# Placing expert 0's rows by matrix products, in a two-layer mixture-of-experts backbone on one Trainium2 core

## The reference, cut to what matters

```python
h2l = modulate(rms_norm(xl, norm_ffn[l]), sh2, sc2)
xl = xl + g2 * moe_ffn(h2l, w_router, b_router, *experts)
# moe_ffn, per token:
#   aff = sigmoid(tok @ w_router); best group of 4 experts; best 2 experts in it -> e_idx, w_sel
#   xs = tok_pad[row_tok]                      # rows sorted by expert, in blocks of 128
#   hb = silu(xb @ w_gate[e]) * (xb @ w_up[e]); ys = hb @ w_down[e]
#   out[token] += ys * row_w
```

## Time and profile before

| | |
|---|---|
| median of the runs | 2365.96 us |
| the profiled execution | 2363.81 us |
| its span in the profile | 2362.2 us |
| PE busy | 88% of the span |
| DVE / ACT / POOL busy | 70% / 49% / 8% |
| mean DMA rate | 267 GB/s |

### The profile page before, as it was taken

The page is one execution under the profiler, slowest core; times in us unless marked ns, Lnnn a source line. Parts: engine busy times, 40 slices in busy tenths (PEclk is TensorE's granted clock), DMA queues, the critical chain, the costliest instruction groups (busy, mean ns, idle before and its releaser), DMA issues. The chain is left out here.

```text
span 2362.2 us, 25910 instructions
## 1 busy us (share of the span) xinstructions
PE 2085.5 (88%) x9496; PEld 1607.6 (68%) x9496; DVE 1651.7 (70%) x1672; ACT 1152.3 (49%) x1088; POOL 180.2 (8%) x245
## 2 busy tenths in 40 slices
PE   5797999999956999999998648989949999999993
PEld 1586656666754888888887237647737888888883
DVE  4575483334645999999998657445648999999994
ACT  0322512122214777777775223514326777777772
POOL 2000000111011000000000100000010000000001
PEclk9798999999977999999999769999959999999996
DMA  8475104766336999999998258137458999999992
GB/s 322 148 244 187 38 1 162 248 217 222 125 151 236 354 392 394 399 388 398 393 397 328 81 174 296 58 112 248 163 220 310 395 391 395 398 387 394 400 392 106
DMA packets 132249, 629.82 MB, mean 267 GB/s; under 512 B 14985, under 2 KB 17173, under 8 KB 75976
## 3 DMA queue, kind: packets, MB, share of 16 engines
q1 hardware_dynamic: 101432, 505.23, 55.6%
q0 software_dynamic: 26992, 118.77, 13.7%
q10 hardware_dynamic: 3744, 4.73, 0.6%
HBM read 596.48 MB, written 32.20 MB: 266 GB/s over the span
## 5 line engine op out<-in xcount | busy, mean ns | idle before, releaser
L1256 DVE TENSOR_TENSOR w_lo<-ring,w_hi 128x2048 fp32r<-128x2048 f32 x384 | 874.0, 2290 | 113.7 <-ACT w_hi L1146 113.5
L1146 ACT ACTIVATE w_hi<-ring 128x2048 fp32r<-128x2048 f32 x384 | 736.9, 1921 | 253.3 <-PE bank L1862 253.3
L1862 PE MATMUL bank<-w_hi,xsT_hi 128*128 128x512 f32 x1024 | 402.0, 393 | 13.5 <-DVE w_lo L1256 10.7
L1862 PE MATMUL bank<-w_lo,xsT_hi 128*128 128x512 f32 x1024 | 400.6, 391 | 0.0
L953 ACT ACTIVATE m_hi<-ring 128x1024 fp32r<-128x1024 f32 (+1 forms) x128 | 130.8, 1031 | 388.7 <-PE bank L1862 330.1
L1862 PE MATMUL bank<-w_hi,xsT_lo 128*128 128x512 f32 x1024 | 317.1, 391 | 0.0
L1256 DVE TENSOR_TENSOR m_lo<-ring,m_hi 128x1024 fp32r<-128x1024 f32 (+1 forms) x128 | 150.7, 1191 | 235.9 <-ACT m_hi L953 234.0
L1862 PE MATMUL bank<-m_hi,hT_hi 128*128 128x512 f32 (+1 forms) x640 | 252.2, 394 | 27.3 <-DVE work L1256 11.5
L1862 PE MATMUL bank<-m_lo,hT_hi 128*128 128x512 f32 (+1 forms) x688 | 265.9, 386 | 0.0
L1862 PEld LDWEIGHTS bank<-w_hi,xsT_hi 128*128 128x128 f32 x1024 | 194.0, 189 | 56.3 <-issue 10.5
L1862 PE MATMUL bank<-m_hi,hT_lo 128*128 128x512 f32 (+1 forms) x592 | 227.4, 384 | 0.0
(11 more groups left out here) (222 smaller groups left out, 2271.6 us busy)
## 6 DMA issues: line engine op xcount, KB each, us to landing
ring<-in_w_exp_gate_dram SPq DMA_DIRECT2D x128, 1024.0 KB, 8.5
ring<-in_w_exp_up_dram SPq DMA_DIRECT2D x128, 1024.0 KB, 6.9
ring<-in_w_exp_down_dram SPq DMA_DIRECT2D x128, 1024.0 KB, 7.8
ring<-in_w_in_dram SPq DMA_DIRECT2D x44, 1024.0 KB, 6.6
work<-in_w_mod_dram POOLq DMA_DIRECT2D x40, 1024.0 KB, 6.1
ys_dram<-work POOLq DMA_DIRECT2D x32, 512.0 KB, 8.1
work<-hp_dram SPq DMA_DIRECT2D x54, 256.0 KB, 3.7
work<-mod_dram POOLq DMA_DIRECT2D x12, 1024.0 KB, 9.8
```

Of the source, the lines that this page charges most:

```text
L1146: nc.scalar.activation(w_hi[:, pos % N_SPLIT, :], raw(i), ACT.Copy).then_inc(hi_done, 1)
L1256: return nc.vector.tensor_tensor(o, a, b, op)
L1862: return nc.tensor.matmul(o, a, b, start=first, stop=last)
```

## The change

Expert 0's rows no longer go through DRAM. `cnt` is turned at once into a zero-one matrix per block of tokens (`place`: token p goes to slot n of expert 0), and PE multiplies the norm's rows, as they lie in SBUF, with it; this places and transposes them in one step, into the same banks 2 and 3 that the transposes used. The slot numbers come from one more product of two constants (job `slots`). Experts 1 to 15 take the scatter and gather as before. ACT and DVE make the first two weight parts before they take expert 0's rows instead of after. PE's wait before the expert phase names the last users of banks 2 and 3 instead of `r` and `tot`. POOL issues the next layer's filter loads after the gathers of experts 1 and 2 instead of ahead of the gather of expert 0, and ACT's `gate(0)` waits for the rows' store.

```diff
@@ plan_jobs
+    job("dve", "slots", l)
     job("dve", "cnt", l)
@@ hybrid_kernel
+        place = mixed[:, 0:512].rearrange("p (t n) -> p t n", t=4)
+        slot_no = mixed[:, 512:640]
@@ POOL
-                if l + 1 < DEPTH:
-                    pool.wait_ge(dve_took, TAKEN[("tot", l)])
-                    for dst, src in filter_weights(l + 1):
-                        pool.dma_start(dst, src).then_inc(filt_loaded[l + 1], 16)
-                    for dst, src in tap_weights(l + 1):
-                        pool.dma_start(dst, src).then_inc(taps_loaded[l + 1], 16)
...
-                for e in range(NE + 2):
+                for e in range(1, NE + 2):
                     if e < NE:
                         if e >= 2:
...
+                    if e == 2 and l + 1 < DEPTH:
+                        pool.wait_ge(dve_took, TAKEN[("tot", l)])
+                        for dst, src in filter_weights(l + 1):
+                            pool.dma_start(dst, src).then_inc(filt_loaded[l + 1], 16)
+                        for dst, src in tap_weights(l + 1):
+                            pool.dma_start(dst, src).then_inc(taps_loaded[l + 1], 16)
@@ ACT
                     act.wait_ge(w_used, ready_at(e, 3) + Wb)
+                    if isinstance(e, int) and e == 0:
+                        for b in range(2):
+                            act.wait_ge(h2_stored[b], 16 * (T_BEFORE[l] + len(T)) // 2)
...
-                take_xs(0, 0)
                 high(0, 0)
                 high(0, 1)
+                take_xs(0, 0)
@@ DVE
+                b = take(("slots", l))
+                nc.vector.tensor_scalar(slot_no, b[:, 0:P], 1.0, None, ALU.add).then_inc(dve_took, 1)
+                dve.wait_ge(dve_took, took[0])
                 dve.wait_ge(sel_ready, l + 1)
+
+                b = take(("cnt", l))
+                nc.vector.tensor_copy(r(11), b[:, 0:w16]).then_inc(dve_took, 1)
+                dve.wait_ge(dve_took, took[0])
+                link(nc.vector.scalar_tensor_tensor(out=rt1[:, 5, 0:nt], in0=r16(11)[:, :, 0], scalar=1.0,
+                                                    in1=r16(9)[:, :, 0], op0=ALU.add, op1=ALU.mult))
+                TT(place[:, 0:nt, :], slot_no.unsqueeze(1).broadcast_to([P, nt, P]),
+                   rt1[:, 5, 0:nt].unsqueeze(2).broadcast_to([P, nt, P]), ALU.is_equal).then_inc(placed, 1)
 
                 link(TT(r(10), r(0), r(9), ALU.mult))
...
-                b = take(("cnt", l))
-                nc.vector.tensor_copy(r(11), b[:, 0:w16]).then_inc(dve_took, 1)
-                dve.wait_ge(dve_took, took[0])
...
-                low_xs(0, 0)
                 low(0, 0)
                 low(0, 1)
+                low_xs(0, 0)
@@ PE
+                b = begin("slots", l)
+                mm(b[:, 0:P], ones, tri, True, True).then_inc(mm_done, 1)
                 pe.wait_ge(sel_ready, l + 1)
...
-                pe.wait_ge(act_took, TAKEN[("r", l, T[-1])])
-                pe.wait_ge(dve_took, TAKEN[("tot", l)])
+                for i in (2, 3):
+                    old = [n for n in order[:DONE[("tot", l)]] if (DONE[n] - 1) % N_BANK == i][-1]
+                    pe.wait_ge(act_took if taker[old] == "act" else dve_took, TAKEN[old])
...
+                def place_first():
+
+                    pe.wait_ge(placed, l + 1)
+                    for half in range(2):
+                        for j in range(4):
+                            for k in range(nt):
+                                rows = h2row[k][:, half * 512:(half + 1) * 512]
+                                s4 = rows.rearrange("p (q i k) -> p q k i", q=2, k=2)
+                                ins = mm(bank[2 + half][:, j * P:(j + 1) * P], s4[:, j // 2, j % 2, :], place[:, k, :],
+                                         k == 0, k == nt - 1)
+                        ins.then_inc(xt_mm, 1)
...
-                turn_xs(0, 0)
+                place_first()
```

More of the change, by code:

```diff
@@ L442, in hybrid_kernel @@
         sel_ready = sem("sel_ready")
+        placed = sem("placed")
         idx_ready = sem("idx_ready")
@@ L2154, in turn_xs @@
                     if isinstance(e, int):
-                        pe.wait_ge(xs_loaded[par], 8 * Lb + 16 * (e // 2 + 1))
+                        pe.wait_ge(xs_loaded[par], 16 * ((NE // 2 - 1 + par) * l + e // 2 + par))
                     else:
-                        pe.wait_ge(xs_loaded[par], (e - par) * 8 + (8 * Lb + 16))
-                    if not (isinstance(e, int) and e == 0):
-                        pe.wait_ge(h_done, e * 2 + 2 * Lb)
+                        pe.wait_ge(xs_loaded[par], (e - par) * 8 + 16 * ((NE // 2 - 1 + par) * l + par))
+                    pe.wait_ge(h_done, e * 2 + 2 * Lb)
                     for half in range(2):
                         turn_rows_of(bank[2 + half], xs[:, par, half * 512:(half + 1) * 512]).then_inc(xt_mm, 1)
+                def place_first():
[8 more added lines that the diff above has]
+                        ins.then_inc(xt_mm, 1)
                 def turn_rows_of(dst, src):
```

## The result

The changed kernel takes 2326.17 us in the median of 4 runs (2322.70 to 2330.60), the kernel before beside it 2365.88 us. The ratio is 0.9837, 95% interval 0.9813 to 0.9861, a gain of 39.7 us. The forecast was 2328.9 us.

The account below looks back on a forecast made before the run. PE was taken to set the pace from expert 0's first product on, so gains of 22.7 and 14.4 us there, together 37.1, gave 2365.96 - 37.1 = 2328.9 us; the 8-in-10 range was 2322 to 2340.

Parts of the forecast that it names:

- First products: Expert 0's first product on PE comes at 707.3 us in layer 0 and 1746.2 in layer 1, gaining 22.7 and 14.4.
- The placement: PE's placement products in layer 0: 64 records, 4 us cold and 6.1 us warm, together 10.1 us.
- the first of the two signs of being wrong: The prediction is wrong if the first products of both layers move by less than 30 us together.
- E: Better than forecast: placement leaves PE's clock high for the first product, up to 2 us per layer, 2325 us; chance 0.10.
- B: Placement on PE stays cold, all 64 records at 0.245 us: first product at 712.5, time 2334.1 us; chance 0.11.
- C: Slower than before: the weight stream becomes the bound over 31 later experts, up to 2382 us; chance 0.03.
- D: Something other than the gather holds the first product, so only the parts ahead count: 2363 us; chance 0.03.
- What moves to POOL's later time: Expert 1's rows in layer 0: gather issued at 715.1, landed 726.1, needed 735.2, leaving 9.1 us of cover.
- second sign of being wrong: The prediction is wrong if the gain at the first products is given back later as idle PE time.
- A: Expert 1's rows come late because scatters run beside DVE's low parts: 2333 to 2347 us, likeliest 2333; chance 0.18.
- Parts made ahead: ACT's high parts cost nothing; DVE's two low parts, 4.50 us, come right after its chain, no longer behind the rows.
- The rule that was weighed: Two-SBUF-input DVE instructions and GpSimd share an interface: whole-part wait, 2347 us, against 0.85 us per scatter, 2333.

Follow-up runs that it names:

- rows1_early: Changed kernel with expert 1's rows gathered by block 0's token numbers before the scatters, so it computes on wrong tokens; 2316.32 us.
- stream_held: Changed kernel with SP's refills of raw weight places held until POOL's table is loaded; 2339.27 us.
- place_only: Changed kernel, but ACT and DVE take expert 0's rows first and make the first two weight parts after them, as before; 2326.4 us.
- rows_first_held: place_only with the hold of stream_held (refills wait until the table is loaded), one run; 2333.96 us.
- the repeats: The changed kernel run twice more without any edit; 2329.88 us and 2334.42 us.
- repeat 2: Second rerun of the changed kernel without any edit; 2334.42 us.
- parts_only: Kernel before with only the first two weight parts made ahead of expert 0's rows on ACT and DVE; 2362.84 us.

## Why the prediction came out as it did

**First products: right.** 23.4 and 14.9 us were gained where 22.7 and 14.4 were forecast. The terms: DVE's chain got 1.77 us longer from `cnt` to `tot`'s maximum (7.22 instead of 5.45 us; forecast 1.96), since the comparison took the 0.69 us of the earlier trace rows, but the next operation started before its end. In layer 1 it was 1.40 (forecast 1.5). The placement took 9.4 us (forecast 10.1), with the clock rising among the records as assumed; in layer 1 all 32 took 5.91 us, well ahead of DVE. The low parts took 4.48 us and `low_xs` 1.28. The slots job cost nothing: DVE did it in 0.28 us and then idled for 1.88 before `cnt`. So the first of the two signs of being wrong, under 30 us at the first products, did not come: it was 38.2.

**E came in part.** The clock is 1.00 from 700 us on, and the first product takes 0.50 us instead of 0.77. In layer 1 it was 0.50 again in the window from 1731, 1.4 us behind the first product, and in `rows1_early` and `stream_held` the first product of layer 1 took 0.79 and 0.80 us, so there this gain isn't sure. `place_only`, where PE idles 4.90 us before the first product instead of 2.19, has it at 0.77 in layer 0, and so has `rows_first_held`; in all ten profiles that have the placement and the parts ahead it is 0.50. So in layer 0 the parts made ahead are what keeps the clock up.

**B, C and D did not come.** The clock rose 3.8 and 4.3 us into the placement. The steady phase has PE busy 80.00 of 80 us, as the earlier trace rows has it, at 391 GB/s (there 401), so the stream never became the bound. And the first products moved.

**The failed step: "What moves to POOL's later time".** It had the gather issued at 715.1 and landed at 726.1, 9.1 us ahead of need. It was issued at 730.79 and landed at 740.27, a stall of 6.28 us, so the second sign of being wrong, gain given back as idle PE time, did come in part. The forecast shifted the chain of before by DVE's 1.96 us and took the scatters (10.00 us), their landing (1.45) and the load of the table (2.27) as they were in the earlier trace rows. They became 16.35, 6.49 and 5.51. Only the gather had a reserve, and by chance: the forecast took it at 11.0 us, the median of all 32, where the gather in the same place had taken 5.84; it took 9.48. The forecast itself had priced that case as A, with a chance of 0.18, and A's terms against what came:

| term of A | forecast | measured (layer 0) |
|---|---|---|
| scatters beside low parts | +6.8 | +6.4 |
| landing of the scatters | +2.3 | +5.0 |
| load of the table | +2.4 | +3.2 |
| gather, issue to landing | 12.7 | 9.48 |
| rows there, us from the start | 739.3 | 740.27 |
| stall of PE | 4 | 6.28 (6.67 and 6.60 in the repeats) |

That A's time for the rows is met to 1 us is luck in part: the gather was issued 4.2 us later than its terms give (726.6), 1.2 of them because the router itself started later, and then took 3.2 us less. Its mechanism is what came, and A should have been the forecast. What spoke for the cover was only a belief that DVE's gaps would let the scatters through. But the first three parts follow each other in DVE's order with `low_xs` alone between them, and the first two start when the scatters do. The net loss is 4.8 us rather than 6.3, because the high clock (E) gives some of it back. 38.2 - 4.8 = 33.4 us, against 37.1.

That the first measured median, 39.7, lies so near to the forecast is luck: the profiled execution gained 33.2, the repeats 32.3 and 27.8, and only the stall in layer 1 (2.3 us of repeat 2) is known of what sets the batches apart. The rest is open.

**Parts made ahead: right on their own path, wrong in the sum.** They save 3.6 and 1.0 us before the first product, and in layer 0 some 2 us behind it by the clock (29.02 us to expert 1's first product in `rows1_early`, 31.05 in `place_only`). They cost the stall. `place_only` shows that the change would gain as much without them, `parts_only` that they are worth nothing alone.

**The rule that was weighed.** A scatter waits for the rest of the low part that is running when it is issued. The first was issued at 702.44 beside a part begun at 702.14. With half of 4.48 us for one part, it ends at 704.38; 704.38 + 0.97 - 702.44 = 2.91, measured 2.92. The second waits until DVE's next instruction starts at 706.54: 1.85, measured 1.84. The other slow ones of this layer (2.21, 1.93 and 2.42 us) come out the same way, each 0.13 us below the sum. The third is issued at 707.80, as `xsT_lo` ends, so it shows nothing. `place_only` does: its second scatter starts 0.34 us into an `xsT_lo`, which has one operand in PSUM, and takes 1.00 us; waiting for the rest of it would have made 1.3. DVE's own parts keep their 2.24 to 2.29 us, also where a scatter was there first: the low part that starts at 708.15, 0.35 us into the third scatter, takes 2.29.

This is what the Trainium skill says ("SBUF — State Buffer", section "Who interferes with whom"): the one that comes first holds the interface for its whole instruction, and with at most one SBUF input DVE does not contend (outside its 2-port modes). The trace agrees where DVE comes first, and with the second statement. That an indirect transfer which comes first holds DVE up is in none of these rows. The mistake was in how I turned the rule into a price. I took "whole part" as 2.25 us for every scatter. The loser pays only what is left of the part, and nothing in the gaps: 6.4 us over eight scatters, 0.8 each.

## What to carry to other kernels

An engine's idle time is free only if its work there touches nobody else's path. Filling DVE's gap with instructions of two SBUF operands, and starting the weight stream 25 us earlier, both landed on POOL's chain of small transfers, which had 9 us to spare by the forecast. When a step comes off the critical path, write down its new due time and cost the chain that must meet it anew, piece by piece, with the durations it has beside its new neighbours. And put what someone waits for first in each order: moving the tokens' weights behind what the scatters and the placed rows need brought the gain to 47.0 and 44.5 us, where the change itself has 27.8 to 39.7.

## What the runs showed of the hardware

- Small transfers pay for a running weight stream. Where the refills run, the landing of layer 0's scatters goes from 1.45 us to between 5.7 and 8.1 (6.49 in the changed kernel), the load of 8 KB from 2.3 to 5.5, the gather from 5.8 to 9.5, of which 1.0 is its issue beside a low part (2.06 instead of 1.02). With the stream held the first two are back at 1.44 and 2.2 us.
- A plain store issued by POOL beside a low part doesn't pay what an indirect transfer pays. DVE's timeline and POOL's in the steady phase of the changed kernel:

```profile
823.20 4.48 DVE L1263 TENSOR_TENSOR w_lo<-ring,w_hi 128x2048 fp32r<-128x2048 f32 x2
```

```profile
823.58 0.55 POOL L847 DMA_DIRECT2D ys_dram<-work  x1 [31.83 <-DVE work L1768]
824.44 1.91 POOL L836 DMA_INDIRECT mixed<-h_dram,idx_exp  x1 [0.30 <-issue]
```

  The store, 0.38 us into the first part, takes 0.55 us; the gather, until that part's end at 825.44 and then 0.97, would take 1.97 and takes 1.91. The other stores of this layer beside a low part take 0.54 to 0.56. The store carries no list of indices in SBUF, the gather does; that this is what makes the difference is not shown.
- With 128-column float32 records the granted clock rose to 1.00 3.8 us (layer 0) and 4.3 us (layer 1) after they began in the changed kernel, and 2.9 to 6.1 us in the other runs with the placement. In layer 0 the 64-column records of `cnt` and `tot` ran right before them for 3.60 us. The 16-column ones kept it at 0.50 for all of 3 us in the kernel before.
